# Draining tile 0 of a product's first column chunk at the end of its own pass, in a two-block transformer kernel on one core

## The reference

```python
for layer in range(2):                      # first stack
    x = x + 0.5 * swiglu(rmsnorm(x), gu_pre, dn_pre)
    x = x + mixer(rmsnorm(x))               # stick-breaking + gated units, or MLA
    x = x + memory_cross_attention(rmsnorm(x), rmsnorm(mem), wq, wkv, wo)
    x = x + 0.5 * swiglu(rmsnorm(x), gu_post, dn_post)
h = x
for i in range(2):                          # second stack
    h = layer_norm(A * h + 0.5 * swiglu(h, w1[i,0], w3[i,0], w2[i,0]), ...)
    h = layer_norm(A * h + mix(h), ...)     # convolution + S5, or sparse attention
    h = layer_norm(A * h + 0.5 * swiglu(h, w1[i,1], w3[i,1], w2[i,1]), ...)
    h = h + (p[i] @ ple_w_proj[i]) * sigmoid(h @ ple_w_gate[i])
```

## Time and profile before

| | us |
|---|---|
| median of 3 runs (lowest, highest) | 2337.58 (2337.45, 2337.99) |
| the profiled execution, its time | 2338.7 |
| its span (first to last instruction) | 2336.9 |
| PE busy, share of the span | 2258.7, 97% |
| DVE busy | 1447.2, 62% |
| ACT busy | 1121.9, 48% |
| POOL busy | 200.0, 9% |
| mean granted TensorE clock | 0.987 |

### The profile page before, as it was taken

How to read it: one execution, slowest core, us unless ns; L and a number is a source line. 1 busy time by engine, 2 the same in 40 slices (tenths; PEclk the granted TensorE clock), 3 DMA queues, 4 the chain that set the end, 5 groups by cost and what they waited for, 6 DMA issues and landing times.

```text
span 2336.9 us, 25939 instructions
## 1 busy us (share of the span) xinstructions
PE 2258.7 (97%) x10458; PEld 1836.4 (79%) x10458; DVE 1447.2 (62%) x1959; ACT 1121.9 (48%) x1667; POOL 200.0 (9%) x235
## 2 busy tenths in 40 slices
PE   8999999999999999999999999979999999989999
PEld 6888877888888887778888887557887888877887
DVE  5655665655565577655556776876556555576556
ACT  6545565544455457554444444134444444364443
POOL 0000000000000020000003951720000000010000
PEclk9999999999999999999999999979999999999999
DMA  7666533565655562426656665225664665525553
GB/s 264 207 183 216 159 121 120 182 188 184 211 189 182 181 192 72 153 87 204 185 184 201 187 189 180 73 65 183 188 183 162 202 188 185 165 82 198 188 182 124
DMA packets 111144, 396.55 MB, mean 170 GB/s; under 512 B 13232, under 2 KB 14000, under 8 KB 110896
## 3 DMA queue, kind: packets, MB, share of 16 engines
q1 hardware_dynamic: 111024, 394.90, 53.0%
HBM read 393.80 MB, written 1.05 MB: 169 GB/s over the span
## 4 chain that ended last, share of the span: by engine, by line
PE 87%; DVE 8%; ACT 3%; DMA 1%; issue 0%; POOL 0%; SPq 0%; DVEq 0%; ACTq 0%
PE bank L547 26%; PE bank L549 26%; PE bank L548 26%; PE bank L595 2%; DVE wlo L1689 2%; PE bank L606 2%; PE bank L664 1%; PE bank L650 1%; PE bank L888 1%; ACT whi L1111 1%; DMA raw<-in_w_ple_g 0%; PE bank L639 0%; DVE bn L1824 0%; DVE X L1854 0%; DVE ds_work L2407 0%
## 5 line engine op out<-in xcount | busy, mean ns | idle before, releaser
L1689 DVE TENSOR_TENSOR wlo<-raw,whi 128x1024 fp32r<-128x1024 f32 (+2 forms) x718 | 872.7, 1252 | 245.2 <-ACT whi L1111 243.4
L1111 ACT ACTIVATE whi<-raw 128x1024 fp32r<-128x1024 f32 (+2 forms) x718 | 720.8, 1049 | 204.5 <-DMA raw<-in_w_w 91.4
L547 PE MATMUL bank<-whi,XH 128*128 128x512 f32 (+2 forms) x1840 | 729.7, 397 | 7.6 <-DVE wlo L1689 6.8
L549 PE MATMUL bank<-whi,XL 128*128 128x512 f32 (+2 forms) x1840 | 716.8, 390 | 0.0
L548 PE MATMUL bank<-wlo,XH 128*128 128x512 f32 (+2 forms) x1840 | 715.9, 389 | 0.0
L547 PEld LDWEIGHTS bank<-whi,XH 128*128 128x128 f32 x1840 | 349.0, 190 | 80.9 <-issue 14.3
L549 PEld LDWEIGHTS bank<-whi,XL 128*128 128x128 f32 x1840 | 348.4, 189 | 72.1
L548 PEld LDWEIGHTS bank<-wlo,XH 128*128 128x128 f32 x1840 | 349.2, 190 | 66.2
L547 PE MATMUL bank<-whi,HH 128*128 128x512 f32 x704 | 279.4, 397 | 0.0
L548 PE MATMUL bank<-wlo,HH 128*128 128x512 f32 x704 | 277.6, 394 | 0.0
L549 PE MATMUL bank<-whi,HL 128*128 128x512 f32 x704 | 277.3, 394 | 0.0
(11 more groups left out here) (411 smaller groups left out, 2106.8 us busy)
## 6 DMA issues: line engine op xcount, KB each, us to landing
raw<-in_w_w SPq DMA_DIRECT2D x264, 512.0 KB, 3.5
raw<-in_w_gu_pre SPq DMA_DIRECT2D x88, 512.0 KB, 3.6
raw<-in_w_gu_post SPq DMA_DIRECT2D x88, 512.0 KB, 3.5
raw<-in_w_dn_pre SPq DMA_DIRECT2D x44, 512.0 KB, 3.5
raw<-in_w_dn_post SPq DMA_DIRECT2D x44, 512.0 KB, 3.5
raw<-in_w_x_kv SPq DMA_DIRECT2D x32, 512.0 KB, 4.0
raw<-in_w_sbg_in SPq DMA_DIRECT2D x20, 512.0 KB, 3.6
raw<-in_w_x_q SPq DMA_DIRECT2D x16, 512.0 KB, 4.7
```

The costliest lines, as they stand in the source:

```text
L547: pe.e.matmul(o, xh, hi[:, k, :], start=kt == 0, stop=False)
L549: m = pe.e.matmul(o, xl, hi[:, k, :], start=False, stop=kt == kts - 1)
L1111: act.e.activation(whi[v % SLOTS][:, 0:n], raw[v % SLOTS][:, 0:n], ACT.Copy).then_inc(*hi_ok.did(v))
L1689: dve.e.tensor_tensor(wlo[v % SLOTS][:, 0:n], raw[v % SLOTS][:, 0:n], whi[v % SLOTS][:, 0:n].bitcast(F32), ALU.subtract).then_inc(*lo_ok.d ...
```

## The change

In the first chunk, "out" for tile 0 is yielded right after tile 0's pass. It stands ahead of flush (1,) and ahead of the four splits and steps of tile 1's pass. "out" for tile 1 comes where both came before. Every later item that needs both tiles is now added with tile 1 alone: the factor (1 in tiles) shown for pe_ffn stands alike on ACT and DVE and for x_kv, x_q, sbg_in and ab_in. The two waits that named the transposes of the product's input follow: each now names those of its own tile, both column pieces.

```diff
@@ schedule
-            if last:
-                yield "out", c, (0,)
+            yield "out", c, (0,)
             if first:
                 yield "flush", (1,)
             for j, (i, k0, nk) in enumerate(rest):
...
             if last:
                 yield "flush", (0,)
-                yield "out", c, (1,)
-        if not last:
+            yield "out", c, (1,)
+        else:
             yield "out", c, (0, 1)
@@ pe_ffn
-            for i in pe_run(gu, lhs_of(key), lambda c, t: [(dve_ok, ("h", gu, c, t))], lambda c, tiles: [(None, ("hidden", n, gu, c))]):
+            for i in pe_run(gu, lhs_of(key), lambda c, t: [(dve_ok, ("h", gu, c, t))], lambda c, tiles: [(None, ("hidden", n, gu, c))] * (1 in tiles)):
...
@@ pe_last
-                if i == 0:
-                    pe_ok.mark(("pleg", l))
+                pass
@@ act_kv, out
-                act_sqrt(st[:, 6:8], ("xk", l, c))
+                if 1 in tiles:
+                    act_sqrt(st[:, 6:8], ("xk", l, c))
@@ act_mla, lora
-                act.wait_ge(pe_ok, ("turn", "mix1", 1, 1))
+                act.wait_ge(pe_ok, ("turn", "mix1", 0, t), ("turn", "mix1", 1, t))
@@ dve_kv, out
+                if 1 not in tiles:
+                    return
                 dve.wait_ge(act_ok, ("xks", l, c, 0), ("xks", l, c, 1))
...
-                for t in tiles:
+                for t in range(2):
@@ dve_last, out of ple_g
-                    dve.wait_ge(pe_ok, ("pleg", l))
+                    dve.wait_ge(pe_ok, ("turn", f"ln{l}2", 0, t), ("turn", f"ln{l}2", 1, t))
@@ POOL, out_q of mla_uq
+                if 0 not in tiles:
+                    return
```

More of the change, by code:

```diff
@@ L676, in pe_kv @@
             yield from pe_run(f"x_kv{l}", lhs_of(f"mem{l}"), lambda c, t: [(dve_ok, ("xk", l, c, t)), (act_ok, ("xv", l, c, t))],
-                              lambda c, tiles: [(None, ("xk", l, c))], late=2)
+                              lambda c, tiles: [(None, ("xk", l, c))] * (1 in tiles), late=2)
         def pe_xk_turn(l, c):
@@ L706, in pe_memory @@
             for i in pe_run(f"x_q{l}", lhs_of(f"xm{l}"), lambda c, t: [(dve_ok, ("xq", l, c, j, t)) for j in range(2)],
-                            lambda c, tiles: [(None, ("xq", l, c))]):
+                            lambda c, tiles: [(None, ("xq", l, c))] * (1 in tiles)):
                 if i in (6, 7):
@@ L792, in after @@
                 return [(act_ok, {0: ("evu", t), 1: ("evg", t), 2: ("evQ", 2, t), 3: ("evQ", 3, t), 4: ("evv", t)}[c])]
-            for i in pe_run("sbg_in", lhs_of("mix0"), after, lambda c, tiles: [(None, ("evqk", c))] if c in (2, 3) else []):
+            for i in pe_run("sbg_in", lhs_of("mix0"), after, lambda c, tiles: [(None, ("evqk", c))] if c in (2, 3) and 1 in tiles else []):
                 step(i)
@@ L919, in after @@
                 return [(dve_ok, ("abc", t))] if c == 2 else [(act_ok, {0: ("abu", t), 1: ("abh", t), 3: ("abg", t)}[c])]
-            later = lambda c, tiles: [(None, ("ab",) + {0: ("u", 0), 2: ("c", 2), 3: ("g", 0)}[c])] if c != 1 else []
+            later = lambda c, tiles: [(None, ("ab",) + {0: ("u", 0), 2: ("c", 2), 3: ("g", 0)}[c])] if c != 1 and 1 in tiles else []
             for i in pe_run("ab_in", lhs_of("ln00"), after, later):
@@ L1058, in pe_last @@
             nxt = "raw1" if l == 0 else "out"
-            for i in pe_run(f"ple_g{l}", lhs_of(f"ln{l}2"), lambda c, t: [(act_ok, ("sig", l, c, t))], pieces(nxt) if l == 0 else nothing, tail=True):
-                if i == 0:
-                    pe_ok.mark(("pleg", l))
+            for _ in pe_run(f"ple_g{l}", lhs_of(f"ln{l}2"), lambda c, t: [(act_ok, ("sig", l, c, t))], pieces(nxt) if l == 0 else nothing, tail=True):
+                pass
         def pe_mem(l, i):
@@ L1206, in gate @@
                                      scale=root[:, t:t + 1] if rooted else 1.0).then_inc(*act_ok.did(("sg", gu, c, t)))
-            for i in act_run(gu, gate, lambda c, tiles: [(None, ("hidden", n, gu, c))]):
+            for i in act_run(gu, gate, lambda c, tiles: [(None, ("hidden", n, gu, c))] * (1 in tiles)):
                 if step:
@@ L1262, in out @@
                                      accum_out=st[:, 6 + t:7 + t]).then_inc(*act_ok.did(("xks", l, c, t)))
-                act_sqrt(st[:, 6:8], ("xk", l, c))
-            yield from act_run(f"x_kv{l}", out, lambda c, tiles: [(None, ("xk", l, c))], late=2)
+                if 1 in tiles:
+                    act_sqrt(st[:, 6:8], ("xk", l, c))
+            yield from act_run(f"x_kv{l}", out, lambda c, tiles: [(None, ("xk", l, c))] * (1 in tiles), late=2)
         def act_memory(l):
@@ L1281, in out @@
                     act_sqrt(st[:, 8 + 2 * t:10 + 2 * t], ("xq", l, c, t))
-            for i in act_run(f"x_q{l}", out, lambda c, tiles: [(None, ("xq", l, c))]):
+            for i in act_run(f"x_q{l}", out, lambda c, tiles: [(None, ("xq", l, c))] * (1 in tiles)):
                 if i in (6, 7):
@@ L1328, in act_even @@
             act_ok.mark(("end", "ev", 0))
-            for i in act_run("sbg_in", out, lambda c, tiles: [(None, ("evqk", c))] if c in (2, 3) else []):
+            for i in act_run("sbg_in", out, lambda c, tiles: [(None, ("evqk", c))] if c in (2, 3) and 1 in tiles else []):
                 step(i)
@@ L1807, in evac @@
                                             ALU.mult).then_inc(*dve_ok.did(("h", gu, c, t)))
-            for i in dve_run(gu, evac, lambda c, tiles: [(None, ("hidden", n, gu, c))]):
+            for i in dve_run(gu, evac, lambda c, tiles: [(None, ("hidden", n, gu, c))] * (1 in tiles)):
                 if step:
@@ L1920, in out @@
                 dve.wait_ge(row_in[f"xk{l}"], 0)
-                for t in tiles:
+                for t in range(2):
                     dve.e.scalar_tensor_tensor(out=XQ[l][:, c % 2, t, :], in0=banks.of[(f"x_kv{l}", c), t][:, 0:256], scalar=st[:, 6 + t:7 + t],
                                                in1=kg, op0=ALU.mult, op1=ALU.mult).then_inc(*dve_ok.did(("xk", l, c, t)))
-            yield from dve_run(f"x_kv{l}", out, lambda c, tiles: [(None, ("xk", l, c))], late=2)
+            yield from dve_run(f"x_kv{l}", out, lambda c, tiles: [(None, ("xk", l, c))] * (1 in tiles), late=2)
         def dve_xk_turn(l, c):
@@ L1959, in out @@
                                                    op0=ALU.mult, op1=ALU.mult).then_inc(*dve_ok.did(("xq", l, c, j, t)))
-            for i in dve_run(f"x_q{l}", out, lambda c, tiles: [(None, ("xq", l, c))]):
+            for i in dve_run(f"x_q{l}", out, lambda c, tiles: [(None, ("xq", l, c))] * (1 in tiles)):
                 if i in (6, 7):
@@ L2055, in dve_even @@
             sp_job("row", "sgu_b", ("end", "ev", 0))
-            for i in dve_run("sbg_in", None, lambda c, tiles: [(None, ("evqk", c))] if c in (2, 3) else []):
+            for i in dve_run("sbg_in", None, lambda c, tiles: [(None, ("evqk", c))] if c in (2, 3) and 1 in tiles else []):
                 step(i)
```

## The result

The changed kernel takes 2354.45 us (median of 4 runs, 2352.51 to 2356.01) against 2337.51 before: a ratio of 1.0075, 95% interval 1.0062 to 1.0087. It is 17 us slower, where I had forecast 13.35 (2350.9, range 2343.0 to 2357.5). A later comparison of the same two kernels gave 2352.53 against 2337.76, ratio 1.0058 (1.0045 to 1.0072). The profiled execution took 2354.7, with a span of 2352.7. The runs of the kernel before that came with the experiments lie between 2330.3 and 2341.3, wider than the first three. A ratio is the recorded estimate over all the other runs of a comparison, so it can differ in the fourth digit from the quotient of the two medians beside it.

The account below looks back on a forecast made before the run. The prediction took PE, 97% busy with unchanged matmuls, to bound the kernel. It summed 7.15 (x_kv0 with clock) + 3.9 (w13 products) + 4.1 (ple_g1) - 1.8 (ple_g0) = 13.35 us slower: 2350.9 us, range 2343.0 to 2357.5.

Parts of the forecast that it names:

- The bound: Whole kernel: PE is busy 97% of the span, 2258.7 us, with matmuls the change neither removes nor speeds up.
- Plain first chunks at 0: First chunks such as gu_post0, sbg_out and x_o: about 1.7 us of cover is left, so they cost 0.
- x_kv0, 5.45: x_kv0's first chunk: the attention's chain through DVE and ACT has no slack and starts later, delaying PE 5.45 us.
- Its clock, 1.7: Behind x_kv0's stall: PE runs at least 3 us at half clock, costing 1.7 us.
- w13_0_1 and w13_1_1, 3.9: Two products behind a LayerNorm: DVE's low piece falls behind tile 0's out, PE waits 1.95 us in each, 3.9.
- ple_g1, 3.1 + 1.0: Kernel's end: PE starts tile 1's pass 3.1 us late behind a longer out, plus 1.0 for the clock.
- ple_g0, -1.8: ple_g0: a new 3.1 us wait replaces an old stall and its half clock; net gain 1.8 us.
- Table loads: ACT in the LayerNorm waits: 1.30 us from load to activation, by the trace, without the skill page's 1.38 us drain.
- (a): Rival: the attention's chain has slack, only LayerNorm waits count; 6.2 us slower, 2343.8; chance 0.14.
- (b): Rival: half clock follows each new stall, short ones too; 20.4 us slower, 2358.0; chance 0.12.
- (c): Rival: DVE's low piece runs ahead of out 0, waits are covered, ple_g0 gains; 5.2 us faster, 2332.4; chance 0.06.
- (d): Rival: the change does not do what it says, all stays under PE's work; 2337.6; chance 0.06.

## Why the prediction was right, point by point

- **The bound** holds: PE is busy at 96%, 5.4 of the 15.8 us are busy time for the same matmuls, and the rest is idle time of PE.
- **Plain first chunks at 0.** Right for gu, w13_0_0, w13_1_0, sbg_in, mla_in, ab_in, c_in, c_out, x_q and x_kv1. All within 0.4 us, the most that I can tell at one place. Wrong for sbg_out, x_o0, mla_out and x_o1, which are 2.45 us of the whole. I costed them by gu_post0, where nothing behind the late splits is urgent. In these four the next chunk is the last, its X is the next product's input, and DVE reaches it behind eight splits. It is the step "or have an out on fewer engines" that failed: the out there has a square on ACT, and by the timelines the splits wait for it.
- **x_kv0, 5.45.** Measured 5.46, 5.47 and, alone, 5.46. The two runs with the out behind a split show the mechanism.
- **Its clock, 1.7.** Mis-sized: 2.28 to 2.64. The bound from the earlier trace rows was for one stretch. Here the lower clock lasts longer, as three windows in a row show (below).
- **w13_0_1 and w13_1_1, 3.9.** Measured 3.84. The lines of ACT and DVE are those of the sum, and moving the out behind the low piece takes all of it away.
- **ple_g1, 3.1 + 1.0.** Measured 3.09, with 1.55 or 0 for the clock: a chance term, and a mean over the two cases was what I had put in.
- **ple_g0, -1.8.** Measured -1.37. First +3.06 and +1.49 (forecast 3.1 and 1.0), then -5.92 (forecast -2.8 and -3.1). The half clock was surer than I had put it.
- **Table loads.** 2325.53 to 2326.83, 1.30 us from load to activation. The drain of about 1.38 us that the Trainium skill, page "ScalarE: Activation LUTs", section "What ACT_TABLE_LOAD costs", adds has no place in these waits, and a sum with it would have been 1.4 us too long at each of the four.
- **The rivals.** (a) fell with the run of x_kv0 alone. (b) came in part: the half clock followed the long stalls, not the 1.7 us ones. (c) fell for this kernel, but its condition was put rightly: with the low piece ahead of the out the waits are covered. Its price, 5.2, was too high for that: 3.44. With tile 1's out moved as well it comes near, 5.9 at the place and 4.7 net. (d) fell.
- **The range.** Its low sum, 9.6, does not use the low bounds named with the terms. With these (0 for x_kv0, 1.4 for the two w13, 2.4 for ple_g1, -2.8 for ple_g0) it would be 1.0. So the low end was narrower than the working behind it. It was not put to the test, since both measurements came out above the forecast.

The errors were nearly all of one sign: 2.45, 0.6 to 0.9 and 0.4 too little, and the two traces end 1.5 and 2.3 below their sums, mostly by chance of the clock elsewhere. So the forecast of 13.35 stands nearer to the measured 14.8 and 16.9 than its terms alone would have it, and that part is luck.

## What to carry to other kernels

When all engines walk one list, moving a drain earlier moves every instruction behind it on the draining engine later, to the end of what it waits for: look for the first one that another engine needs soon, and put the drain behind that one. No run here gained by a bank that came free sooner; the one gain, in ple_g0, came from X, which the drain makes and PE waits for. A wait that vanishes may only be hidden by a new lateness upstream, so undo the lateness before crediting the gain.

## What the runs showed of the hardware

Windows at the lower clock: behind x_kv0's stall, behind ple_g0's and behind ple_g1's, changed kernel (PE busy, and PEclk third from the end):

```profile
297.00:300.00 3.00, 0.00 (x0) 0.00 (x0) 0.70 (x1) 3.00 (x3) 0.00 (x0) 0.88 0.63 175
300.00:303.00 3.00, 1.82 (x5) 1.22 (x5) 3.00 (x5) 2.77 (x8) 0.00 (x0) 0.50 0.00 0
303.00:306.00 3.00, 3.00 (x9) 2.37 (x8) 2.69 (x8) 2.70 (x4) 0.00 (x0) 0.50 0.00 0
1805.00:1808.00 3.00, 3.00 (x8) 2.33 (x9) 2.52 (x3) 0.00 (x1) 0.00 (x0) 0.50 0.99 358
2330.00:2333.00 3.00, 3.00 (x10) 2.30 (x9) 3.00 (x4) 1.70 (x2) 0.00 (x0) 0.54 0.18 64
```

All three stalls (4.26, 2.81 and 2.82 us) were followed by the lower level, the first for longer than the others; there the clock fell while PE still stood idle (0.88 in a window without a matmul). In the second trace of the same kernel the stall in ple_g1 was not followed by it, although the wait was as long. The kernel before has a like case, this wait ahead of 333.5:

```profile
PE bank L547 <- DVE ev_ol L1745: 2.0, 1, 2.0
```

It is followed by full clock there, and in nine of the eleven other traces the shift grows by 1.6 us right behind the same wait of 2.02 us. So near 2 to 3 us of idle PE the fall of the clock is not settled by the length of the stall alone. A fall behind these stalls cost about 1.6 us, the one behind x_kv0's stall 2.3 to 2.6. The spread between executions of the kernel before goes with the granted clock: its mean was 0.990 to 0.993 in the runs of 2332.6 us and less, and 0.985 to 0.987 in those above 2340.

I had not expected the spread of the run with x_kv0 alone: nine of its twelve runs lie between 2346.3 and 2348.8 us at a mean granted clock of 0.983 to 0.986, three between 2337.4 and 2339.0 at 0.989 or 0.990. Its profile is one of the nine. What is different in the three is open.
